# A routed-expert layer of 512 tokens: half of the tokens by dense products over streamed expert units, half by gathered rows that VectorE adds up

## What is computed

```python
def peer_layer(h, w_q, sub_keys, u_tab, v_tab):        # h: 512 tokens x 1024
    q = (hf @ w_q).reshape(T, 8, 2, 128)
    s = jnp.einsum('thpd,hpnd->thpn', q, sub_keys)      # 8 heads, 2 sides, 128 keys
    sc, idx = lax.top_k(s, 16)
    cand = sc[:, :, 0, :, None] + sc[:, :, 1, None, :]  # 16 x 16 sums
    cidx = idx[:, :, 0, :, None] * 128 + idx[:, :, 1, None, :]
    top_sc, pos = lax.top_k(cand, 16)                   # 16 experts per head
    eidx = jnp.take_along_axis(cidx, pos, axis=-1)
    gate = jax.nn.softmax(top_sc, axis=-1)
    ...
        act = jax.nn.gelu(jnp.einsum('thkd,td->thk', u_tab[eb], hb), approximate=False)
        return jnp.einsum('thk,thkd->td', gb * act, v_tab[eb])
# h = h + g2 * peer_layer(u2, ...);  return rms_norm_2(h, final_g)
```

## Time and profile before

| | us |
|---|---|
| time, median of 3 | 3456.01 (3455.7 to 3457.72) |
| span of the profiled execution | 3452.1 |
| PE busy | 3142.6 (91%) |
| DVE busy | 2087.5 (60%) |
| ACT busy | 1062.6 (31%) |
| POOL busy | 1917.9 (56%) |
| moved over DMA | 741.68 MB, of it 536.90 MB by the gathers |

### The profile page before, as it was taken

How to read it: one execution, slowest core, us unless ns; L and a number is a source line. 1 busy time by engine, 2 the same in 40 slices (tenths; PEclk the granted TensorE clock), 3 DMA queues, 4 the chain that set the end, 5 groups by cost and what they waited for, 6 DMA issues and landing times.

```text
span 3452.1 us, 34902 instructions
## 1 busy us (share of the span) xinstructions
PE 3142.6 (91%) x12254; PEld 2099.6 (61%) x12254; DVE 2087.5 (60%) x3701; ACT 1062.6 (31%) x2577; POOL 1917.9 (56%) x1198
## 2 busy tenths in 40 slices
PE   7999999999999999999999999999978787777776
PEld 5778778887766888868777677544433333333332
DVE  5764453336764433479556776777667676666654
ACT  4564441112165211120132432333333332333222
POOL 4545259997403899968767565444444444434432
PEclk9999999999999999999999999999999999999999
DMA  4430022232311222323413124999999999999997
GB/s 164 171 134 1 13 86 98 97 120 74 134 62 49 90 95 96 115 71 124 140 62 115 50 80 172 421 421 419 422 415 412 421 421 421 421 421 420 421 421 299
DMA packets 108994, 741.68 MB, mean 215 GB/s; under 512 B 11816, under 2 KB 12968, under 8 KB 20776
## 3 DMA queue, kind: packets, MB, share of 16 engines
q0 software_dynamic: 73728, 536.90, 37.5%
q1 hardware_dynamic: 31488, 196.25, 16.2%
q10 hardware_dynamic: 3624, 6.56, 0.5%
HBM read 731.28 MB, written 8.39 MB: 214 GB/s over the span
## 4 chain that ended last, share of the span: by engine, by line
PE 63%; DMA 21%; DVE 8%; ACT 4%; issue 2%; POOL 2%; DVEq 0%; POOLq 0%; ACTq 0%
DMA arena<-in_peer_uv,rstd 15%; PE bank L1298 13%; PE bank L1299 13%; PE bank L1300 13%; PE bank L1814 8%; DMA weight_ring<-in_peer_uv,rstd 3%; DMA normed<-in_peer_uv,rstd 2%; DVE arena L3295 2%; PE bank L1829 1%; PE bank L1744 1%; PE bank L1726 1%; PE bank L1612 1%; PE bank L1490 1%; PE bank L1245 1%; PE bank L1500 1%
## 5 line engine op out<-in xcount | busy, mean ns | idle before, releaser
L1155 POOL DMA_INDIRECT arena<-in_peer_uv,rstd x419 | 456.4, 1089 | 622.0 <-PE bank L1814 570.3
L3295 DVE CUSTOM_DVE_ANT_0 arena<-arena,branch 128x1024 f32<-128x1024 f32 x419 | 510.5, 1225 | 333.5 <-DMA arena<-in_peer_uv,rstd 327.5
L1300 PE MATMUL bank<-split_arena 128*128 128x512 f32 x1776 | 695.1, 391 | 0.0
L1066 POOL TENSOR_TENSOR split_arena<-weight_ring,ones 128x1024 fp32r<-128x1024 f32 x204 | 506.6, 2483 | 151.0 <-PE bank L1300 99.3
L1298 PE MATMUL bank<-split_arena 128*128 128x512 f32 x1392 | 546.6, 393 | 5.6 <-DVE split_normed L2697 2.5
L1299 PE MATMUL bank<-split_arena 128*128 128x512 f32 x1392 | 542.3, 390 | 0.0
L1068 POOL TENSOR_TENSOR split_arena<-weight_ring,split_arena 128x1024 fp32r<-128x1024 f32 x204 | 519.3, 2545 | 16.0
L1814 PE MATMUL bank<-arena,row_diagonals 128*128 128x512 f32 x836 | 397.8, 618 | 92.0 <-ACT row_diagonals L2425 91.7
L1814 PE MATMUL bank<-arena,level_mask 128*128 128x512 f32 x840 | 392.0, 608 | 75.0 <-ACT level_mask L2425 74.7
L1300 PEld LDWEIGHTS bank<-split_arena 128*128 128x128 f32 x1776 | 334.0, 188 | 73.6
L1035 POOL TENSOR_TENSOR split_arena<-weight_ring,split_arena 128x1024 fp32r<-128x1024 f32 x54 | 129.5, 2406 | 401.2 <-ACT split_arena L1980 349.3
(11 more groups left out here) (490 smaller groups left out, 4921.4 us busy)
## 6 DMA issues: line engine op xcount, KB each, us to landing
weight_ring<-in_w_up SPq DMA_DIRECT2D x32, 1024.0 KB, 4.9
weight_ring<-in_w_down SPq DMA_DIRECT2D x32, 1024.0 KB, 4.9
weight_ring<-in_w_in SPq DMA_DIRECT2D x32, 1024.0 KB, 5.0
weight_ring<-in_ada_w SPq DMA_DIRECT2D x24, 1024.0 KB, 4.9
weight_ring<-in_w_in_a SPq DMA_DIRECT2D x12, 1024.0 KB, 6.4
weight_ring<-in_w_out SPq DMA_DIRECT2D x12, 1024.0 KB, 6.9
weight_ring<-in_w_in_b SPq DMA_DIRECT2D x10, 1024.0 KB, 5.9
arena<-in_peer_uv,rstd POOLq DMA_INDIRECT x419
```

The costliest lines, as they stand in the source:

```text
L1066: pool.tensor_tensor(hi, part, bc_mid(ones[:], DT), ALU.mult).then_inc(split_hi, 1)
L1155: pool.indirect_dma_start(row_slots[slot_of[r]], None, a["peer_uv"], bass.IndirectOffsetOnAxis(ap=experts[n % 2][:, c:c + 1], axis=0)).the ...
L1300: return pe.matmul(psum[t.bank][:], hi, a_lo[k], start=False, stop=last)
L3295: dve.tensor_tensor_reduce(row, row, h_tok[:, r // NE, :], 1.0, 0.0, ALU.mult, ALU.add, dots[:, i % 4, j:j + 1]).then_inc(dot_ready, 1)
```

## The change

It splits the tokens. For the lower 256 (blocks 0 and 1) the rows are gathered as before (NROW = 256), but the weighted sum is made by DVE: ACT scales the GELU of a dot by its gate, and DVE adds weight times v row to an accumulator in SBUF. The diagonal matrices and PE's row sums are gone.

For the upper 256 (blocks 2 and 3) every expert is computed. All experts with the same second key form a unit: `peer_ut[m]` (their 128 u rows, turned, 0.5 MB) and `peer_vd[m]` (their 128 v rows, 0.5 MB). An up unit is eight products [128 experts x 256 tokens]; ACT writes its GELU to `weights`. That is multiplied by a gate matrix, which is zero where a token has not chosen an expert, and a down unit makes four products of 512 columns which add up in four banks over all 128 units. The gate matrix of a token is the product of two one-hot matrices of its 128 choices (first key; second key times gate), made by DVE and POOL, 8 tokens a step. `weights` holds 64 of 128 units; so the stage runs as 64 up items, 32 gate steps, 64 pairs of a down and an up item, 8 "back" steps that multiply the second half of the gates (stored to DRAM by ACT and loaded again by SP), and 64 down items. Items pass through four places that lie over the residual X, which SP stores to DRAM before and loads into `normed` at the end. All searches of blocks 0, 2 and 3 now lie in the first 61 steps, those of block 1 in the mixed steps. The second normalization on DVE moves ahead of the first full search.

```diff
+        STEPS = [("item", n) for n in range(WHALF)] + [("gate", q) for q in range(NGATE)]
+        G_AT, MIX_AT = WHALF, len(STEPS)
+        STEPS += [("item", n) for n in range(WHALF, 3 * WHALF)]
+        BACK_AT = len(STEPS)
+        STEPS += [("back", i) for i in range(NGATE // LOADS)]
+        LAST_AT = len(STEPS)
+        STEPS += [("item", n) for n in range(3 * WHALF, 4 * WHALF)]
...
+        for s in range(61):
+            search_steps += [s] * (2 if 12 <= s < 44 else 1)
+        search_steps += range(MIX_AT + 2, MIX_AT + 2 + 64)
...
-        first_at = {10: (5, 0), 11: (5, 1), 18: (6, 0), 19: (6, 1), 22: (7, 0), 23: (7, 1)}
+        first_at = {8: 5, 17: 6, 18: 7}
+        for j, at in ((0, 0), (1, 4), (2, 9), (3, 13), (7, 19), (4, 23), (5, 27), (6, 31)):
+            for y in range(4):
+                query_at[at + y] = (j, y)
...
+        step_us = [6.1 if s < 35 else 3.6 if s < G_AT else 3.0 if s < MIX_AT else 3.5 for s in range(len(STEPS))]
+        for a0, a1, rows in ((3, G_AT, 64), (G_AT, MIX_AT, 10), (MIX_AT, BACK_AT, 120), (BACK_AT, LAST_AT, 2), (LAST_AT, LAST_AT + 58, 60)):
...
+        row_places = [(arena[:, W_AT + 3 * E:W_AT + 4 * E], 0, 24), (arena[:, W_AT + 4 * E:W_AT + 5 * E], 0, 32),
+                      (arena[:, W_AT + 5 * E:W_AT + 6 * E], 0, 40), (arena[:, W_AT + 6 * E:W_AT + 7 * E], 0, 48),
+                      (pq_flat[:, 0:E], 23, None), (ring[:, 0, :], 31, None), (ring[:, 1, :], 36, None),
+                      (pq_flat[:, 2 * E:3 * E], 39, None), (pq_flat[:, 3 * E:4 * E], 41, None), (pq_flat[:, E:2 * E], MIX_AT, None)]
...
+            def load_item(n):
+                value, m = ITEMS[n]
+                if n < RAWS:
+                    if n == 0:
+                        sp.wait_ge(x_saved, 16)
+                        sp.wait_ge(scaled_ready, 2 * DT)
+                else:
+                    sp.wait_ge(item_done, n - RAWS + 1)
+                sp.dma_start(raws[n % RAWS], a["peer_vd" if value else "peer_ut"][m]).then_inc(raw_landed[n % RAWS], 16)
...
             def gather(r):
+                if before is not None:
+                    pool.wait_ge(row_added, before + 1)
...
+            def second_ones(q):
+                for x in range(GTOK // 2, GTOK):
+                    m = pool.tensor_scalar(one_second[q % 2][:, x, :], iota_key, index_t[b][:, 1, at:at + 1],
+                                           index_t[b][:, 2, at:at + 1], ALU.is_equal, ALU.mult)
...
-                    for t, c in zip(row_sums[n], (0, 512)):
-                        m = pe.matmul(psum[t.bank][:], diag[i % 2][:, j, :], row_slots[slot_of[r]][:, D + c:D + c + 512],
-                                      start=r % NE == 0, stop=r % NE == NE - 1)
...
+            def up_unit(n, j):
+                for k in range(DT):
+                    m = pe.matmul(psum[t.bank][:, 0:DENSE], blk(raws[n % RAWS], k), H[:, k, DENSE:], start=k == 0, stop=k == DT - 1)
+            def down_unit(n, m):
+                elif m == WHALF:
+                    pe.wait_ge(gate_used, NGATE)
+                for b in range(2):
+                    for c in range(2):
+                        x = pe.matmul(psum[2 * b + c][:], blk(weights[:, m % WHALF, :], b), raws[n % RAWS][:, 512 * c:512 * (c + 1)],
+                                      start=m == 0, stop=m == NKEY - 1)
+            def gate_products(q):
+                for x in range(GTOK):
+                    for half, t in enumerate(gate_tiles[q]):
+                        m = pe.matmul(psum[t.bank][:, x * WHALF:(x + 1) * WHALF], one_first[q % 2][:, x, :],
+                                      one_second[q % 2][:, x, half * WHALF:(half + 1) * WHALF], start=True, stop=True)
...
+            def activate(j):
+                act.activation(weights[:, j % WHALF, :], psum[t.bank][:, 0:DENSE], ACT.Gelu).then_inc(bank_out[t.bank], 1)
+            def keep_gates(q):
+                act.activation(gate_out[q % 2].rearrange("p (j t) -> p j t", t=GTOK), psum[t.bank][:].rearrange("p (t j) -> p j t", t=GTOK),
+                               ACT.Copy).then_inc(bank_out[t.bank], 1)
+                act.dma_start(weights_dram[q], gate_out[q % 2]).then_inc(gate_stored[q % 2], 16)
+            def weigh_row(r):
+                act.wait_ge(row_dot, r + 1)
+                act.activation(w, dots[:, r % RING8:r % RING8 + 1], ACT.Gelu).then_inc(row_gelu, 1)
+                act.wait_ge(row_gelu, r + 1)
+                act.activation(w, w, ACT.Copy, scale=gates[n][:, c:c + 1]).then_inc(row_weight, 1)
...
+            def one_hots(q):
+                dve.tensor_tensor(one_first[q % 2], bc_mid(iota_key, GTOK), bc_last(index_t[b][:, 0, GTOK * t:GTOK * (t + 1)], NKEY),
+                                  ALU.is_equal)
+                for x in range(GTOK // 2):
+                    m = dve.tensor_scalar(one_second[q % 2][:, x, :], iota_key, index_t[b][:, 1, at:at + 1],
+                                          index_t[b][:, 2, at:at + 1], ALU.is_equal, ALU.mult)
+            def gate_weights(q):
+                dve.tensor_tensor(w, w, psum[t.bank][:].rearrange("p (t j) -> p j t", t=GTOK), ALU.mult).then_inc(bank_out[t.bank], 1)
+            def later_weights(q):
+                dve.wait_ge(gate_landed[q % LOADS], 16 * (q // LOADS + 1))
+                dve.tensor_tensor(w, w, gate_back[q % LOADS].rearrange("p (j t) -> p j t", t=GTOK), ALU.mult).then_inc(gate_used, 1)
+            def add_row(r):
+                dve.wait_ge(row_weight, r + 1)
+                    m = dve.scalar_tensor_tensor(row_acc[n], row, w, row_acc[n], ALU.mult, ALU.add)
...
+            for s, (kind, v) in enumerate(STEPS):
+                for r in rows_at[s - 2] if s >= 2 else ():
+                    add_row(r)
+                for r in rows_at[s]:
+                    dot_row(r)
+                for k in piece_at.get(s, ()):
+                    next(walks[k], None)
...
+            add_rows(2)
+            finish_rows(0)
+            finish_rows(1)
+            add_rows(3)
+            finish_rows(2)
+            finish_rows(3)
```

More of the change, by code:

```diff
@@ L576, in build @@
+        v_tiles = [item_tile(2 * NKEY - 1, b) for b in range(4)]
         q_f = region(0, LH)
@@ L1139, in _, with gather @@
                 split_half(u, h, out_w, ((landed[u.slot], 16 * u.load), place), u.own + h + 1)
-            for r in range(NROW):
+            def gather(r):
                 n, c = divmod(r, NE)
@@ new lines, in _ @@
+            for s, (kind, v) in enumerate(STEPS):
+                if kind == "gate":
+                    second_ones(v)
+                for r in gathers_at[s]:
+                    gather(r)
+                if s == 1:
+                    pool.wait_ge(half_done, 2 * (wo_units[-1].u + 1))
+                    ch.link(pool.iota(iota_key_i, [[1, NKEY]], base=0, channel_multiplier=0))
+                    pool.tensor_copy(iota_key, iota_key_i).then_inc(iota_ready, 1)
+                    pool.wait_ge(iota_ready, 1)
@@ new lines, in _ @@
+            for s, (kind, v) in enumerate(STEPS):
+                if kind == "gate":
+                    gate_products(v)
+                elif kind == "item" and ITEMS[v][0]:
+                    down_unit(v, ITEMS[v][1])
+                elif kind == "item":
+                    up_unit(v, ITEMS[v][1])
+                if s in first_at:
+                    for h in range(2):
+                        first_half(first_at[s], h)
+                if s in query_at:
+                    query_piece(*query_at[s])
+                if s in turn_at:
+                    token_turn(*turn_at[s])
+                if s in score_at:
+                    key_scores(*score_at[s])
+                if s in index_at:
+                    b = index_at[s]
+                    pe.wait_ge(turn_in, sum(k[0] >= 2 and searched[k] <= searched[2 + b, 3] for k in SEARCHES))
+                    turn(index_tiles[b], [firsts[2 + b], seconds[2 + b], gates[2 + b]])
+                if s == GAIN_AT:
@@ L3213, in search @@
                 have(dve, peer_scores[n][g])
[L3214 removed]
+                if n == 1 and g == 0:
+                    for x in gate_stored:
+                        dve.wait_ge(x, 16 * NGATE // 2)
+                yield from best16(2 * nh, top_v[:, halves, :], top_i[:, halves, :], score_of[n][:, halves, :], left_keys)
                 ch.link(dve.tensor_copy(top_f[:, halves, :], top_i[:, halves, :]))
@@ new lines, in dot_row @@
+            def dot_row(r):
+                n = r // NE
+                row = row_places[row_place[r]][0][:, 0:D]
+                if r >= RING8:
+                    dve.wait_ge(row_gelu, r - RING8 + 1)
+                if r % NE == 0:
+                    for t in tok_turns[n]:
+                        have(dve, t)
+                dve.wait_ge(row_landed[row_place[r]], 16 * row_fill[r])
+                dve.tensor_tensor_reduce(row, row, h_tok[:, n, :], 1.0, 0.0, ALU.mult, ALU.add,
+                                         dots[:, r % RING8:r % RING8 + 1]).then_inc(row_dot, 1)
```

604 lines of the change are left out of this document (362 added, 242 removed).

## The result

The changed kernel takes **3575.1 us** (median of 4 runs, 3573.2 to 3576.3) where the kernel before takes 3456.9 (median of 4): ratio 1.0343, 95% interval 1.0328 to 1.0357. It is 118 us slower. The prediction said 3389 and a range up to 3505; it was wrong in sign and outside its range.

A forecast was written before the change was run, and what follows sets the result against it. The last 1300 us were taken as bound by transfers. Stage terms 2148 + 372 + 6 + 128 + 458 + 34 + 225 + 14 = 3385, plus 3.9, gave 3389 us; range 3285 to 3505.

The forecast's parts named there:

- the price of the gate products: Gate stage, PE: 16 products of 64 columns with weight loads, 2.9 to 3.6 us a step, taken as 3.2.
- The upper end of 6.3 us a step: Gate stage: step length if DVE's compare slowed to 4.0 us beside POOL; 4.0 a step was taken, 128 us in all.
- Rival A: PE sets every stage, with the gate step at 3.2 us; 3292 us in all, chance 0.17.
- The price of GpSimd's operation: Gate stage: four small POOL operations a step at some 0.29 us each, 1.2 us together.
- The contention that the prediction charged to DVE: Gate stage: POOL's operations delay DVE's compare; half of POOL's 1.2 us added, making 4.0 us a step.
- The flight of the gathers in stage 1: Stage 1: reused places leave about 6.2 us for a gather against 6.0 needed; 11 us added, stage 372.
- rival B: Stage 1: gathers come too late, each of 35 reuses stalling DVE by 4.7 us; 3543 us in all, chance 0.10.
- The mixed stage as one average: Mixed stage of 128 items: transfers 458 us at 421 GB/s, above PE's 442 and DVE's 352; 458 taken.
- Rival C: Mixed and last stages: mixed traffic reaches only 351 GB/s, the mixed stage taking 550 us; 3516 in all, chance 0.10.
- the estimate with 341 GB/s for the units: Mixed stage: an item takes 1.54 us instead of 1.25, the stage an estimated 37 us more.
- Last stage and back steps: After the mixed stage: back steps 34 us (ends 28, 45); last stage 225, from PE 225 and bytes 229 less 15.
- Rival D: All steps: chains through ACT don't overlap, 0.3 us hand-over in each of 296 steps, +89; 3478 us, chance 0.12.

The follow-up runs named there:

- the last variant: Against the best form that was run: 14 instead of 10 rows in the gate stage, 56 instead of 60 in the last, spread over 61 units; 3443.9 us.
- the best form that was run: Changed kernel with 128-column gate products, dots behind search pieces, block 1's pieces every third mixed step, six second one-hots on DVE, two on GpSimd; 3437.2 us.

## Why the prediction was wrong

**The step that failed most: the price of the gate products.** "No row shows 64 columns ... so 2.9 to 3.6 us a step; I take 3.2." All rows of short records that it used lie where PE was at the higher clock. In the stage made of nothing but short records the clock stayed at 0.50, and a step took 6.83. Of the 91 us that this term missed, the wider product gave back 59 and a clock partly restored 26, without fewer gate products. The upper end of 6.3 us a step was put down to DVE contention; no end allowed for PE at its lower clock, though a stretch of the trace of before already has a granted clock below 1. Rival A named PE as the bound, but at the same 3.2 us. What keeps the clock low in such a stage stays open.

**The price of GpSimd's operation** was taken from another kind of operation, 289 ns. The operation itself, one line of a source view (count, then shortest / median / longest ns):

```profile
L1293 POOL TENSOR_SCALAR branch<-arena,masks x128: 780/798/4228, 2562.1 to 2779.4; 128x128 f32<-128x128 f32 x128
```

798 ns in the median, up to 4228 at the longest. It cost nothing in the changed kernel, where PE's step covered it, and set the stage as soon as PE was relieved. The contention that the prediction charged to DVE is there, but on the other side. DVE's compare of 1024 columns takes 1218 ns in the median beside GpSimd's operations and 1218 in the run without them. Of the 128 operations of GpSimd, 32 lasted over 1 us, and each of them ran beside a compare, an add or a dot of DVE, which in 31 cases was running already; together they lasted 52 us over 0.78 each, and DVE's operations beside them cover 58 us. The other 96 lasted 0.86 us at most. Four operations with DVE idle, then one that waited, and DVE beside it:

```profile
2571.09 3.11 POOL L1293 TENSOR_SCALAR branch<-arena,masks 128x128 f32<-128x128 f32 x4
...
2584.73 2.76 POOL L1293 TENSOR_SCALAR branch<-arena,masks 128x128 f32<-128x128 f32 x1
...
2584.49 1.28 DVE L3561 SCALAR_TENSOR_TENSOR weight_ring<-weight_ring,row_gelu 128x1024 f32<-128x1024 f32 x1
2585.69 1.22 DVE L3512 TENSOR_TENSOR mem_values<-arena,masks 128x1024 f32<-128x1024 f32 x1
```

The Trainium skill, page "SBUF — State Buffer", section "Who interferes with whom", says that a DVE operation with two inputs in SBUF and a GpSimd operation that reads SBUF contend, and that the order of issue decides which of the two is blocked. The trace agrees, with GpSimd as the one that waits.

**The flight of the gathers in stage 1.** "it fits by a hair; I add 11 us". This was rival B in a milder form: DVE waited 53.2 us in 19 places, not 165 in 35. The mechanism was seen and under-priced: the 11 us should have been about 50. What the prediction missed is that the order inside a step decides it: with the dots behind the pieces the stage took 371, next to the 372 of the sum, whose 11 us then fit the 13.4 us of waits for landings that are left.

**The mixed stage as one average.** "PE 442, DVE 120 x 2.4 + 64 = 352" compares sums over 128 steps, but the search pieces stand in its first part alone, one in every step: 2.4 x 0.94 + 1.9 = 4.2 us of DVE where PE needs 3.44. There DVE was busy 146 of 150 us. The rest of the miss is rate, 378 and 405 GB/s in the two parts rather than 421, and one stall of 12.5 us in which PE waited for an up unit while transfers were full. Rival C, 351 GB/s for mixed traffic, was wrong, and so was the estimate with 341 GB/s for the units: full slices stand at 417.

**Last stage and back steps.** The same averaging: a unit with a gather beside it is 1.57 MB, 3.76 us at 418 GB/s (in the last variant 16 units with 16 gathers took 60 us, 3.75 each), one without is PE's 3.43. GpSimd issues 54 gathers inside the stage, so 54 of the first and 10 of the second are 238 us; the sum over bytes (229 - 15) and the sum over PE (225) are both smaller than this sum of the larger ones. It also gives a reason why the two runs that moved rows gained so little: with 48 and 50 gathers inside the stage it comes out 1 to 2 us shorter, since a gather less gives back only 3.76 - 3.43 = 0.33 us, and 241.9 and 240.0 were measured against 242.5. This is an estimate that the three runs fit; none was made to test it. The back steps took 43 because DVE's 26.9 us of work waits for the reloaded halves (12.9 us for one of the two buffer groups, above, and 2.8 for the other); the bounds of 28 to 45 held.

**What was right.** The start (1 us), the tail (1 us), the bytes, the add of 1024 columns (1.28 us predicted, 1278 ns measured), DVE's load of stage 1 (328 of the 333 us named). Rival D, hand-overs of 0.3 us in every step, is not what happened: with dots moved the stage met the sum that overlaps them.

The idea itself, fewer bytes for more work on PE and DVE, is worth 19 us in the best form that was run, under a third of the 67 predicted.

## What to carry to other kernels

Price short matrix products at both levels of PE's clock; a stage that consists only of them may stay at the lower one while the profile calls PE fully busy, and then wider products, even wasted ones, shorten it. Sum the larger of the engines' times step by step rather than comparing stage totals, since a load that is uneven inside a stage is not averaged out. Where a buffer is reused right after its release, look at the order inside the step: put the work that needs the landing last.

## What was not expected of the hardware

- 32 f32 records of 64 columns, each with its own weight load, took 6.83 us at a granted clock of 0.50 and 3.52 us at full clock. At 0.50 PE was busy for 218.6 us without a gap, and the clock did not rise. One 512-column product a step lifted the mean clock of the stage from 0.50 to 0.82; with 16 records of 128 columns a step in place of the 32 it was 0.75, though PE was busy only 94 of 160 us.
- A 128-column tensor_scalar with two scalars took 798 ns (median) on GpSimd; on DVE one lasted 340 to 390 ns, and back to back they cost 0.27 us each.
- GpSimd's operations were held up by DVE's adds, dots and compares, by up to 3.4 us for one (4228 ns instead of some 780); DVE's were not held up (compare 1218 ns with and without).
- Transfers of gathers and of 0.5 MB units together reached 417 to 418 GB/s in full slices, next to the 421 of gathers alone.
